# Pooling products move behind the next block's first piece, and a tile's halves are added ahead of the split

## What is computed

```python
hn = rmsnorm(h, mix_norm_pre)
proj = hn @ w_in                       # columns: z 1024, xbc 1536, dt 32, u 1024
z, xbc, dt_raw, u = split(proj)
y_ssd = ssd_mixer(z, xbc, dt_raw, ...) # convolution, 16 heads in two directions,
                                       # gated: y * silu(z), normed in two groups
# pool_mixer(u, w, scale): four groups g of 256 channels, windows 2, 4, 8, 16
mixed = window_mean(u) - u
y_pool = einsum("blgc,gcd->blgd", mixed, w) * scale
mix = concatenate([y_ssd, y_pool]) @ w_out
h = h + rmsnorm(mix, mix_norm_post)
```

## Time and profile before

| | us |
|---|---|
| median of 3 runs | 2367.84 |
| lowest and highest | 2367.78, 2368.92 |
| the profiled execution, its own time | 2367.74 |
| its span, first to last instruction | 2366.0 |
| PE busy in the span | 2351.8 |
| DVE busy | 1622.6 |
| ACT busy | 1217.5 |
| POOL busy | 395.6 |
| PE waiting for DVE's sums, 110 to 215 us (two of `ev`, one of `X`) | 2.2 and 0.9 |

### The profile page before, as it was taken

How to read it: one execution, slowest core, us unless ns; L and a number is a source line. 1 busy time by engine, 2 the same in 40 slices (tenths; PEclk the granted TensorE clock), 3 DMA queues, 4 the chain that set the end, 5 groups by cost and what they waited for, 6 DMA issues and landing times.

```text
span 2366.0 us, 30059 instructions
## 1 busy us (share of the span) xinstructions
PE 2351.8 (99%) x11878; PEld 1981.0 (84%) x11878; DVE 1622.6 (69%) x2043; ACT 1217.5 (51%) x1647; POOL 395.6 (17%) x336
## 2 busy tenths in 40 slices
PE   9999999999999999999999999999999999999999
PEld 7878898888888888888788888887888888888887
DVE  7898578779877777775755556657666655666656
ACT  7866464445544444575655555535444444444442
POOL 1262016326424224300000000001000000000000
PEclk9999999999999999999999999999999999999999
DMA  8446655665666666665556465565665666656654
GB/s 297 156 146 197 213 178 185 199 190 172 213 203 191 188 191 205 202 200 176 180 180 211 153 198 165 164 188 166 193 182 182 221 185 195 180 179 189 187 179 125
DMA packets 122941, 444.05 MB, mean 188 GB/s; under 512 B 13744, under 2 KB 15408, under 8 KB 122288
## 3 DMA queue, kind: packets, MB, share of 16 engines
q1 hardware_dynamic: 122800, 442.12, 59.4%
HBM read 439.97 MB, written 2.10 MB: 187 GB/s over the span
## 4 chain that ended last, share of the span: by engine, by line
PE 95%; DVE 2%; ACT 1%; issue 0%; DMA 0%; SPq 0%; DVEq 0%; ACTq 0%
PE bank L834 94%; DVE wlo L1733 1%; ACT whi L1256 0%; PE bank L983 0%; DVE hT L1736 0%; DVE hn L1736 0%; PE bank L1242 0%; PE bank L1168 0%; ACT hT L1425 0%; PE bank L1190 0%; DMA hT<-in_xT 0%; DVE ev L1736 0%; ACT L1431 0%; DVE xa L1733 0%; DVE xa L1736 0%
## 5 line engine op out<-in xcount | busy, mean ns | idle before, releaser
L1733 DVE TENSOR_TENSOR wlo<-raw,whi 128x1024 fp32r<-128x1024 f32 (+2 forms) x811 | 1037.8, 1287 | 646.9 <-ACT whi L1256 644.6
L1256 ACT ACTIVATE whi<-raw 128x1024 fp32r<-128x1024 f32 (+2 forms) x813 | 847.0, 1048 | 873.2 <-PE bank L834 840.7
L834 PE MATMUL bank<-xa,whi 128*128 128x512 f32 (+1 forms) x2688 | 841.8, 395 | 5.6 <-DVE xa L1736 2.3
L834 PE MATMUL bank<-whi,xa 128*128 128x512 f32 x2048 | 636.1, 392 | 2.2 <-DVE wlo L1733 1.8
L834 PEld LDWEIGHTS bank<-xa,wlo 128*128 128x128 f32 x2656 | 497.7, 188 | 115.1
L834 PE MATMUL bank<-xa,wlo 128*128 128x256 f32 (+1 forms) x2656 | 521.1, 278 | 0.0
L834 PEld LDWEIGHTS bank<-whi,xa 128*128 128x128 f32 x2048 | 379.6, 188 | 79.6 <-DVE wlo L1733 2.4
L834 PE MATMUL bank<-whi,xb 128*128 128x512 f32 x1416 | 436.9, 390 | 0.0
L834 PEld LDWEIGHTS bank<-xa,whi 128*128 128x128 f32 x2688 | 411.3, 188 | 14.8 <-DVE wlo L1733 4.7
L834 PE MATMUL bank<-wlo,xa 128*128 128x512 f32 x1024 | 399.1, 390 | 0.0
L834 PEld LDWEIGHTS bank<-whi,xb 128*128 128x128 f32 x1416 | 264.8, 188 | 55.3 <-DVE wlo L1733 0.5
(11 more groups left out here) (288 smaller groups left out, 1595.4 us busy)
## 6 DMA issues: line engine op xcount, KB each, us to landing
raw<-in_w SPq DMA_DIRECT2D x803, 512.0 KB, 3.7
hT<-in_ln_rows SPq DMA_DIRECT2D x2, 2048.0 KB, 8.8
raw<-in_w SPq DMA_DIRECT2D x9, 256.0 KB, 2.9
S<-in_x SPq DMA_DIRECT2D x4, 512.0 KB, 8.2
hT<-in_x SPq DMA_DIRECT2D x1, 2048.0 KB, 8.1
out<-S SPq DMA_DIRECT2D x8, 256.0 KB, 2.6
hT<-in_xT SPq DMA_DIRECT2D x3, 512.0 KB, 6.7
X<-in_post SPq DMA_DIRECT2D x2, 768.0 KB, 5.4
```

Of the source, the lines that this page charges most:

```text
L834: return pe.matmul(o, w, x, start=start, stop=stop, skip_group_check=True)
L1256: act.activation(hi, r, ACT.Copy).then_inc(*w_high(i))
L1733: return dve.tensor_tensor(o, x, y, op)
```

## The change

Two things change.

First, the pooling products' place. A new helper `around(outer, inner)` begins the outer block and then the inner one, puts the outer block's first piece, then the inner block's only piece, then the outer block's other three. Pooling product 0 now stands behind pool 3's first piece, 1 behind z 0's, 2 behind z 2's, 3 behind z 4's. The outer block's tile numbers now come before those of the product that it holds. `pool_out_split` follows one round after the product, as before.

Second, the place of two sums in DVE's round. The sums of every pool block and of every z block (not only z 0) are in the first pass, ahead of the split of u + 5. Pooling products' sums stay behind it.

```diff
--- before.py
+++ after.py
@@ -132,6 +132,14 @@
             for b, (_, _, _, mat, col) in zip(pair, blocks):
                 u = use(b, mat, col, *k, first=k == full[0], last=k == full[-1])
         return [u - 1, u]
+
+    def around(outer, inner):
+        b, c = (begin(*o[:3]) for o in (outer, inner))
+        for i, (k0, n) in enumerate(full):
+            u = use(b, *outer[3:], k0, n, first=i == 0, last=k0 + n == KT)
+            if i == 0:
+                v = use(c, *inner[3:], 0, 2)
+        return u, v
 
     def flush(u):
         for i, (v, phase, v0, seq, step) in enumerate(placed):
@@ -258,14 +266,24 @@
         if c < 8:
             for j in range(2):
                 late(e + (8 if c == 0 else 6) + j, "xnat", c + j)
+    def pool_out(g):
+        return "pool_out", g, ("pin", g), f"pool{g}", 0
+
     for g in range(4):
-        e = block("pool", g, xa0, "w_in", 2592 + 256 * g, full)
+        pool = "pool", g, xa0, "w_in", 2592 + 256 * g
+        if g == 3:
+            e, v = around(pool, pool_out(0))
+            late(v + 1, "pool_out_split", 0)
+        else:
+            e = block(*pool, full)
         late(e + 6, "pool_split", g)
-        if g > 1:
-            e = block("pool_out", g - 2, ("pin", g - 2), f"pool{g - 2}", 0, [(0, 2)])
-            late(e + 1, "pool_out_split", g - 2)
     for c in (0, 2, 4, 6):
-        e = block("z", c, xa0, "w_in", 128 * c, full)
+        z = "z", c, xa0, "w_in", 128 * c
+        if c < 6:
+            e, v = around(z, pool_out(1 + c // 2))
+            late(v + 1, "pool_out_split", 1 + c // 2)
+        else:
+            e = block(*z, full)
         late(e + 1, "z_silu", c)
         late(e + 2, "z_gate", c)
         late(e + (2 if c == 6 else 3), "z_square", c)
@@ -274,9 +292,6 @@
             late(n, "z_norm", c // 4)
             late(n + 1, "z_split", 4 * (c // 4))
             late(n + 2, "z_split", 4 * (c // 4) + 2)
-        if c < 4:
-            e = block("pool_out", 2 + c // 2, ("pin", 2 + c // 2), f"pool{2 + c // 2}", 0, [(0, 2)])
-            late(e + 1, "pool_out_split", 2 + c // 2)
     ends = {"in": len(uses) - 1}
     n = len(uses)
     ends["mix"] = natural_out("mix", ("xb",), "w_out", pairs(8, 10, 12, 14, 0, 2, 4, 6), 2,
@@ -1898,6 +1913,15 @@
                     q.wait_ge(*piece_tile.of("tile", n))
                     add_halves(conv_pad(c, j)[:, 2:258], bank[n % 4]).then_inc(*vec_evac("tile", n))
 
+            def pool_add(b):
+
+                g = b.arg
+                for j in range(2):
+                    n = b.tile + j
+                    q.wait_ge(*(pool_val.of("pool", g - 2, j, "y") if g >= 2 else vec_val.of("tap", 6 if g else 10, j, 4)))
+                    q.wait_ge(*piece_tile.of("tile", n))
+                    add_halves(upads[g % 2][j][:, 8:264], bank[n % 4]).then_inc(*vec_evac("tile", n))
+
             def z_add(b):
 
                 c = b.arg
@@ -1915,7 +1939,9 @@
                 for step, *k in at[u]:
                     if step == "conv" and k[0].arg in (0, 2):
                         conv_add(k[0])
-                    elif step == "z" and k[0].arg == 0:
+                    elif step == "pool":
+                        pool_add(k[0])
+                    elif step == "z":
                         z_add(k[0])
                 if 0 <= u < N - AHEAD and u not in HELD_BACK:
                     split(u + AHEAD)
@@ -2011,13 +2037,6 @@
                             q.wait_ge(*side.of("y", h))
                             stt(S1[:, c, :], S1[:, c, :], pc("ssd_d", c), bank[6][:, 0:T], ALU.mult,
                                 ALU.add).then_inc(*vec_val("y", c))
-                    elif step == "pool":
-                        g = k[0].arg
-                        for j in range(2):
-                            n = k[0].tile + j
-                            q.wait_ge(*(pool_val.of("pool", g - 2, j, "y") if g >= 2 else vec_val.of("tap", 6 if g else 10, j, 4)))
-                            q.wait_ge(*piece_tile.of("tile", n))
-                            add_halves(upads[g % 2][j][:, 8:264], bank[n % 4]).then_inc(*vec_evac("tile", n))
                     elif step == "pool_split":
                         g, = k
                         for j in range(2):
@@ -2041,8 +2060,6 @@
                             q.wait_ge(*x_high.of("xb", i))
                             stt(xb[:, i, T:2 * T], ev[:, 4 + j, :], pc("pool_scale", 2 * g + j), f32(xb[:, i, 0:T]),
                                 ALU.mult, ALU.subtract).then_inc(*x_low("xb", i))
-                    elif step == "z" and k[0].arg:
-                        z_add(k[0])
                     elif step == "z_norm":
                         g, = k
                         q.wait_ge(*act_evac.of("z_norm", g))
```

## The result

The changed kernel takes 2376.18 us (median; 2374.6 to 2378.82), the kernel before beside it 2367.91. The ratio is 1.0034, 95% interval [1.0026, 1.0043]. It is slower, by 8.3 us, twice the forecast of 4.0, and outside the range. The profiled execution took 2376.29, 8.55 more than that of before.

What follows compares the result with a forecast made beforehand. The prediction took PE's waits to bound the kernel, with DVE setting the pace from 130 to 164 us. New turns of 9.40 us less the old 5.39 gave +4.0 on the median 2367.84: 2371.8 us, range 2367.3 to 2374.6.

Steps and rivals of the forecast that it cites:

- What bounds the kernel: PE's waits are the measure; four turns through pooling and z blocks cost 5.39 us; DVE paces 130 to 164 us.
- what stands behind a moved sum: Behind pool 2's sum, splits and weights of heads 6 and 7 queue; PE needs none for some us; costed at nothing.
- The turn that goes: At pool 3, pooling product 0 now stands behind its first piece, hiding pool 2's two sums: -0.66 us.
- The lag: DVE waits for PE at pool 2's sum and is 1.85 us later than before behind it and its queued work.
- z 0's and z 2's turns: Pool 3 to z 0 and z 0 to z 2, same banks and a late DVE: cost 3.14 and 3.66 us.
- z 4 and z 6: Turns z 2 to z 4 and z 4 to z 6: DVE in time, 1.30 us each; z 6 at most 2.08.
- Sum: New turns 3.14 + 3.66 + 1.30 + 1.30 = 9.40, less 5.39, is +4.0 us: 2371.8.
- Rival (b): Head 6's weights, now beside POOL, take 3.23 instead of 1.39; lag grows 1.84: +5.8, 2373.6 us; chance 0.26.
- Rival (c): TensorE's clock drops after the wait at z 2, a piece costing 1.9 more: +5.9, 2373.7 us; chance 0.05.
- (a): DVE makes up the lag, so all four turns cost the floor of 1.30: -0.2, 2367.6 us; chance 0.22.
- (d): Block ends and starts overlap at the four turns, so the stalls go without a price: -5.4, 2362.4 us; chance 0.03.
- The range: Whole kernel: 2367.3, just below the case of DVE catching up, to 2374.6, one us above that of slow head 6 weights.

Runs made afterwards that it cites:

- experiment 10: The kernel before with one step moved: pool 0's sum ahead of the split of its round; 2370.93 us, ratio 1.0012.
- experiment 3: The changed kernel with the sums of pool 0 and pool 1 put back behind the split; 2374.67 us, ratio 1.0026.
- experiment 4: The changed kernel with POOL starting pool 0's window sums only when head 3's weights are written; 2375.1 us, ratio 1.0029.
- experiment 5: The changed kernel with eight unread products of 512 between pool 3's last and z 0's first; 2377.73 us, ratio 1.0039.
- 8: The changed kernel, all its sums early, with two tile numbers left out ahead of each z block (other banks); 2372.42 us, ratio 1.0017.
- 7: The changed kernel with pool 0's and pool 1's sums late and two tile numbers left out ahead of each z block; 2369.16 us, ratio 1.0004.
- experiment 9: The changed kernel with pool and z sums late, two tile numbers left out at each z block, pooling products behind the second piece; 2365.26 us.
- experiment 6: The changed kernel with pool and z sums back in their old place and two tile numbers left out ahead of each z block; 2365.44 us.
- experiment 2: The changed kernel with the late sums of pool and z blocks back behind the split, leaving only the products' new place; 2371.85 us.
- experiments 1 to 4: experiment 2, experiment 3, experiment 4, and first the kernel before with only its pool and z sums moved ahead of the split, 2373.85 us.

## Why the prediction was wrong, point by point

- **What bounds the kernel.** That PE's standing still is the measure held, and so did the pace of DVE. But I began to read at 130 us. The change moves pool 0's sum too, at 105 us, and I left it with the words that it "starts without a wait, since DVE is well behind PE there". It does start without a wait. **The step that failed is the one on what stands behind a moved sum**: "Queued behind that wait are the splits, the weights of heads 6 and 7 and the pooling tiles' splits; PE needs none of them for some us yet". I asked who is behind the *wait* at pool 2, and not who is behind each *sum*. A DVE that is "well behind PE" is exactly the one whose weights have little slack (0.9 us at head 3). At its place this costs 4.1 us in the changed kernel, and +3.1 for the whole kernel in experiment 10; experiment 3 showed that some of it comes back elsewhere when the wait goes. Of pool 1's sum I said that it starts "about where it did"; behind the stall, DVE was early there and stood idle for 1.84 us ahead of it.
- **The same sentence at heads 6 and 7.** The rows here showed the contrary of "some us yet": PE waits 1.03 for head 7's weights. Before they were ready at 138.5 for products at 140.96, 2.5 us of slack, which the wait of 1.92 and head 6's 3.09 used up.
- **The turn that goes.** Right: no wait at pool 3, -0.66.
- **The lag.** Right: DVE idles 1.92 ahead of pool 2's sum, 1.8 was said. From this sum to pool 3's are 16.67 us (134.09 to 150.76); the forecast had 16.49 (130.31 to 146.8).
- **z 0's and z 2's turns.** 2.28 and 2.53 instead of 3.14 and 3.66. The sum of the stage was near all the same: the rest of z 0's stands at heads 6 and 7 (1.10 + 2.28 = 3.38), the rest of z 2's in the slow pairs behind z 0 (1.53), since DVE's pace sets when the sum at the end comes. 1.10 + 2.28 + 1.53 + 2.53 = 7.44 against 6.80.
- **z 4 and z 6.** Right: 1.36 and 1.37 against 1.30. That z 6 could cost as much as 2.08 fell away.
- **Sum.** 9.4 was forecast for the new turns, 10.2 came (7.44 + 1.36 + 1.37); the rest, 4.1, is heads 2 and 3, a term that the sum didn't have. No pooling product waited, so what I costed at nothing there was right.
- **Rival (b).** Its row came true and its price didn't: head 6's weights take 3.09 beside POOL, but the lag at pool 3's sum grew by 0.2 only. POOL's total is nearly the same (399.0 us of busy time against 395.6), as I had put against it. The rule of the Trainium skill (page "SBUF — State Buffer", section "SBUF: two separate sides") that the two engines lock each other out held at the place where I had not asked for it: head 3's weights, 1.40 beside a POOL at rest in experiment 4, 3.09 and 3.10 beside a working one. In this stage it cost time where PE waited for just that operation.
- **Rival (c).** I put it at z 2 with 0.05. The granted clock did fall to the lower level in mid-kernel, behind heads 2 and 3 (0.79 in 108 to 114 us) and behind z 0 (0.67 in 151 to 155 us), and not at z 2 (1.00 in 168 to 171 us, with a wait of 2.00). By the Trainium skill, page "TensorE: Matmul & The Clock Gate", section "Part 1: The HAM clock gate", a PE that idles falls to half its clock; the trace agrees, with 1.05 us for a pair behind the wait at z 0 and 0.63 where experiment 5 filled that wait. By experiment 5's one profiled execution this low clock behind z 0 cost nothing. Behind heads 2 and 3 it wasn't tried alone, so how much of the 4.11 there is the clock's is not shown.
- **Rivals (a) and (d).** Fell: no turn in the same banks was free, and DVE didn't make up its lag.
- **The range.** Its upper end rested on (b) alone. A second place at which an early sum meets weights of no slack was not among the cases.

What stays open is how much of the changed kernel's 8.3 us belongs to each place, since a loss at one place changes those behind it. Pool 0's early sum costs 3.1 us in the kernel before (3.4 in the stage); pool 0's and pool 1's together cost 3.3 with other banks (8 less 7; 5.3 in the stage) and 1.5 in the changed one (2.6 in the stage), since there DVE's lateness takes back part of what PE gains. Each figure from the stage rests on one execution of a kernel. Also open is what decides behind which wait the clock falls.

## What to carry to other kernels

Moving a step forward in an in-order queue delays everything between its new and its old place. List each of these operations with its consumer's start less its own end; one with less slack than the moved step's time is the price, and if the moved step also sets off an engine beside which these operations are slow, add that. A wait removed from an engine that another one paces can come back later (4.1 us removed and 2.6 kept in experiment 3, nothing gained in experiment 9), so count the pacing engine's work before counting the wait. Two blocks in a row in the same accumulator banks cost at least 1.36 us at each turn in every kernel here that had them; to leave out two tile numbers ahead of each z block was worth 5.6 us (experiment 6 against 2, each against its own before), which made a kernel 2.4 us faster than the one before.

## What the runs showed of the hardware

- A head's four DVE operations with two SBUF inputs took 1.40 us beside a POOL at rest (experiment 4) and 3.09 and 3.10 beside a working one (changed kernel, experiment 10), and up to 3.30 in the kernel before, at 153.28 us. Values between occur too: 2.37 at 166.94 in the kernel before, where POOL stops at 168.5. The sums, which read PSUM, took 1.27 to 1.29 everywhere.
- The granted clock fell behind waits of 2.41 and 1.72 us, and stayed full behind one of 2.00 in the same execution. In experiment 3 the same wait of 1.72 at z 0 left it full, and one of 2.27 at z 2 brought 0.50; in experiment 5 the same 2.27 at z 2 left it full. The length of one wait doesn't tell it.
- The changed kernel's runs spread over 4.2 us (2374.6 to 2378.82), those of before over 1.5 beside it and 3.0 beside experiments 1 to 4, and those of experiment 6, which has no wait over 1.2, over 1.6. Why is not shown.
